# The recurrent solve in 64x64 blocks: one inverse per block pair instead of products on the right-hand sides

## What is computed

```python
def time_step(state, inp):            # state: 8 heads x 64 x 64
    rt, wt, ktt, vt, kht, at = inp
    sk = jnp.einsum('bhvk,bhk->bhv', state, kht)
    state = (state * wt[:, :, None, :]
             - sk[..., None] * (at * kht)[:, :, None, :]
             + vt[..., None] * ktt[:, :, None, :])
    return state, jnp.einsum('bhvk,bhk->bhv', state, rt)
...
_, y = lax.scan(time_step, state0, (tm(r), tm(w), tm(kt), tm(v), tm(kh), tm(a)))
```

## Time and profile before

| | us |
|---|---|
| median of 3 runs | 2790.49 (2789.77 to 2793.28) |
| the profiled execution, whole | 2793.99 |
| its span, first to last instruction | 2792.1 |
| TensorE busy in it | 2194.2 |
| VectorE busy | 660.1 |
| ScalarE busy | 368.9 |
| mean granted clock of TensorE | 0.894 |

### The profile page before, as it was taken

One profiled execution on the slowest core, in us unless ns is written; L12 is line 12 of the kernel. 1 busy time (PEld: TensorE's weight loads), 2 busy tenths in 40 slices (PEclk: granted clock), 3 DMA queues, 4 the chain that ended last, 5 costly groups with the idle time before them and its releaser, 6 DMA issues. The chain is left out here.

```text
span 2792.1 us, 31787 instructions
## 1 busy us (share of the span) xinstructions
PE 2194.2 (79%) x13296; PEld 1373.5 (49%) x13297; DVE 660.1 (24%) x1432; ACT 368.9 (13%) x743; POOL 59.4 (2%) x96
## 2 busy tenths in 40 slices
PE   7887769987769968899766666699688997666665
PEld 5563436653338647688422232286477884222222
DVE  4541114621111253453200000022532112000001
ACT  1510011510010031201100000000311011000000
POOL 0200000200000000000000000000000000000000
PEclk9999999999889989999888788899898998878887
DMA  9349997239993410286699999944100446999997
GB/s 389 121 186 428 428 428 322 91 138 429 428 428 153 165 60 1 99 334 246 275 428 428 429 428 428 427 181 155 56 1 1 157 154 286 427 428 428 429 428 314
DMA packets 55834, 779.42 MB, mean 279 GB/s; under 512 B 6840, under 2 KB 7096, under 8 KB 8120
## 3 DMA queue, kind: packets, MB, share of 16 engines
q1 hardware_dynamic: 55736, 778.02, 66.9%
HBM read 776.95 MB, written 1.05 MB: 279 GB/s over the span
## 5 line engine op out<-in xcount | busy, mean ns | idle before, releaser
L1747 PE MATMUL bank<-ring,arena 128*32 128x512 f32 x3136 | 498.3, 772 | 337.8 <-DMA ring<-in_w_exp 334.0
L1747 PEld LDWEIGHTS bank<-ring,arena 128*32 128x32 f32 x3136 | 101.6, 126 | 726.4 <-DMA ring<-in_w_exp 493.8
L1772 PE MATMUL bank<-ring,arena 128*32 128x512 f32 x1568 | 197.0, 641 | 70.1 <-DMA ring<-in_w_exp 47.3
L885 PE MATMUL bank<-xnT,ring 128*128 128x256 f32 x960 | 212.2, 384 | 9.5 <-ACT xnT L368 9.5
L1927 DVE TENSOR_TENSOR arena<-bank,arena 128x256 f32<-128x256 f32 (+1 forms) x33 | 18.3, 554 | 788.1 <-PE bank L1747 561.3
L885 PEld LDWEIGHTS bank<-xnT,ring 128*128 128x128 f32 x960 | 185.3, 193 | 36.9 <-issue 11.2
L1478 PE MATMUL bank<-xnT,ring 128*128 128x256 f32 x768 | 178.9, 387 | 10.3 <-PEq L1013 10.3
L1478 PEld LDWEIGHTS bank<-xnT,ring 128*128 128x128 f32 x768 | 149.5, 195 | 33.2 <-issue 11.9
L1717 PE MATMUL bank<-arena 128*128 128x256 f32 x592 | 145.8, 402 | 3.6 <-DVE arena L1938 3.6
L1717 PEld LDWEIGHTS bank<-arena 128*128 128x128 f32 x592 | 115.6, 201 | 63.1 <-issue 47.7
L1772 PEld LDWEIGHTS bank<-ring,arena 128*32 128x32 f32 x1568 | 50.6, 113 | 186.6 <-issue 96.2
(11 more groups left out here) (339 smaller groups left out, 2235.7 us busy)
## 6 DMA issues: line engine op xcount, KB each, us to landing
ring<-in_w_exp SPq DMA_DIRECT2D x288, 2048.0 KB, 25.7
arena<-in_w_ada SPq DMA_DIRECT2D x24, 2048.0 KB, 11.2
ring<-in_w_in SPq DMA_DIRECT2D x20, 2048.0 KB, 20.9
ring<-in_w_merge SPq DMA_DIRECT2D x18, 2048.0 KB, 8.2
ring<-in_w_o SPq DMA_DIRECT2D x8, 2048.0 KB, 11.6
ring<-in_w_conv SPq DMA_DIRECT2D x6, 2048.0 KB, 26.4
ring<-in_w_rest SPq DMA_DIRECT2D x2, 1696.0 KB, 26.1
small<-in_small SPq DMA_DIRECT2D x2, 1440.0 KB
```

The source lines that it names most:

```text
L885: last = nc.tensor.matmul(o[:, T * j:T * j + T], w[:, k, col:col + P], xnT[:, k, :], start=k == 0, stop=k == KT - 1)
L1747: last = nc.tensor.matmul(o[rows(e), :], Xw[:, k, rows(e)], ring[:, slot(n), at:at + MW], start=k == 0, stop=k == KT - 1)
L1772: last = nc.tensor.matmul(o[rows(e), :], hidT[:, j, rows(e)], ring[:, slot(n), at:at + MW], start=j == 0, stop=j == ft - 1)
```

## The change

The solve no longer goes by groups. A unit is now a head h and a half c of the token tile, that is 64 tokens (two chunks), and all matrices of a unit are 64x64 with 32x32 blocks on their diagonal. Half c lies on partitions 64c to 64c+63 for operands and for outputs. A step does all 16 units of a token tile, eight heads and two halves, and the two token tiles alternate.

The rounds no longer touch the right-hand sides. With G set to A - 1 (`less_unit`), a round r squares `low` and multiplies the transposed `low` with [power | G] side by side (`round_`, 64x128 in rounds 1 and 2), and VectorE copies the new power and adds the other half to G (`made`). After five rounds G is the negative inverse; `solved` applies it once, `finish` applies the queries' parts into one accumulation, and `turn_back` turns the finished tiles back with 16 transposes, whose results ScalarE copies to `y_rwkv` and VectorE adds to `qrT`. ScalarE also takes the values' products and half of the evacuations. `keys` and `values`, the products of `kdT`, lie between the rounds. Three masks and an unused table leave the constants and two masks and a unit of 64 columns come in; some operands now lie in `small`, behind and in what the stage before has used up. All other stages are as before.

TensorE, in the first solve before: the first group from its start to its second round.

```diff
-put("before", same & (p[:, None] < p[None, :]))
-put("upto", same & (p[:, None] <= p[None, :]))
-put("after", same & (p[:, None] > p[None, :]))
+at = (p % HD)[:, None]
+to = np.arange(HD)[None, :]
+same = at // CH == to // CH
+put("before_upto", np.concatenate([same & (at < to), same & (at <= to)], 1))
+put("past", same & (at > to))
+put("unit", at == to)
-put("start", np.tile((np.arange(T) % CH == 0)[None, :], (P, 1)))
...
-    masks = cst[:, CONST["before"][0]:CONST["upto"][1]]
-    groups = [(t, h) for t in range(TT) for h in (0, 4)]
...
-            for g, (t, h0) in enumerate(groups):
-                if g:
-                    pe.wait_ge(fin_taken, 2 * g)
-                    pe.wait_ge(pow_ready, 7 * g)
...
-                for r in range(5):
...
-                    if r < 4:
-                        b0 = 2 * (r % 2)
-                        for which in ((0, 1) if r < 3 else (1,)):
-                            for i in range(4):
-                                a, b = (top(i), low(i)) if which == 0 else (low(i), top(i))
-                                last = nc.tensor.matmul(bank[b0 + which][:, P * i:P * i + P], a, b, start=True, stop=True)
-                            last.then_inc(sq_done, 1)
-                    pe.wait_ge(x_ready, 6 * g + r + 1)
-                    for i in range(4):
...
-                        last = nc.tensor.matmul(o, top(i), X5[:, 4 * t + (h0 + i) // 2, :, i % 2, :], start=True, stop=True)
-                    last.then_inc(x_prod, 1)
...
+    b_pairs, k_pairs, b_masked, k_masked, unit_ready, low_made, top_made, low_ready, top_ready, g_ready = (
+        sem(f"sol_{n}") for n in ("bpairs", "kpairs", "bmasked", "kmasked", "unit", "lowmade", "topmade", "low", "top", "g"))
+    akv_made, akv_taken, x_made, x_act, x_dve, fin_made, fin_act, fin_dve, fin_turned = (
+        sem(f"sol_{n}") for n in ("akv", "akvtaken", "x", "xact", "xdve", "fin", "finact", "findve", "finturned"))
+    spare_at = SMALL2
+    def wide(x, n):
+        return x.rearrange("p (h s) -> p h s", h=n)
+    B1 = [ar(6144, HEADS, P), ar(16896, HEADS, P)]
+    K1 = [ar(13824, HEADS, P), wide(small[:, spare_at:spare_at + 1024], HEADS)]
+    low = [[ar(7168, HEADS, HD), ar(11776, HEADS, HD)], [wide(small[:, spare_at + 1024:spare_at + 1536], HEADS), ar(12288, HEADS, HD)]]
+    TG = [wide(small[:, 0:1024], HEADS), ar(8704, HEADS, P)]
+    fin = [small[:, 0:1024].rearrange("p (q d) -> p q d", q=4), ar(8704, 4, 2 * P)]
+    units = [(h, c) for h in range(HEADS) for c in range(2)]
+    def rows(c):
+        return slice(HD * c, HD * c + HD)
+    def part(h):
+        return slice(HD * (h % 2), HD * (h % 2) + HD)
+    def x_out(b, h, c):
+        at = 256 * (h // 2 % 2)
+        return bank[b + h // 4][rows(c), at:at + 256].rearrange("p (w i d) -> p w i d", w=2, i=2)[:, :, h % 2, :]
+            def tokens(t, c):
+                return slice(P * t + HD * c, P * t + HD * c + HD)
+            def pairs(t, x, banks):
+                for h, c in units:
+                    j = h // 2
+                    last = nc.tensor.matmul(bank[banks[h % 2]][rows(c), P * j:P * j + P], x[part(h), j, tokens(t, c)],
+                                            qrT[part(h), j, t, :, HD * c:HD * c + HD], start=True, stop=True)
+                return last
+            def lower(t):
+                for h, c in units:
+                    j = h // 2
+                    last = nc.tensor.matmul(bank[4 * t + 2 + h % 2][rows(c), HD * j:HD * j + HD], qrT[part(h), j, t, 0, HD * c:HD * c + HD],
+                                            bT[part(h), j, tokens(t, c)], start=True, stop=True)
+                return last
+            def round_(t, r):
+                top = B1[t] if r == 0 else TG[t]
+                lo = low[t][r % 2]
+                if r == 0:
+                    pe.wait_ge(b_masked, 4 * t + 4)
+                else:
+                    pe.wait_ge(low_ready, 2 * r - 1 + t)
+                    if r < 4:
+                        pe.wait_ge(top_ready, 2 * min(r, 3) - 1 + t)
+                if r < 4:
+                    for h, c in units:
+                        last = nc.tensor.matmul(bank[4 * t + 2][rows(c), HD * h:HD * h + HD], top[rows(c), h, 0:HD], lo[rows(c), h, :], start=True, stop=True)
+                    last.then_inc(low_made, 1)
+                if r == 1:
+                    pe.wait_ge(unit_ready, t + 1)
+                if r >= 2:
+                    pe.wait_ge(g_ready, 2 * (r - 2) + t + 1)
+                a, b = (0, HD) if r == 0 else (0, P) if r < 3 else (HD, P)
+                for h, c in units:
+                    at = P * (h % 4)
+                    last = nc.tensor.matmul(bank[4 * t + h // 4][rows(c), at + a:at + b], lo[rows(c), h, :], top[rows(c), h, a:b], start=True, stop=True)
+                last.then_inc(top_made, 1)
+            def keys(t):
+                if t == 0:
+                    pe.wait_ge(b_masked, 8)
+                else:
+                    pe.wait_ge(akv_taken, 1)
+                pairs(t, kdT, (3, 7)).then_inc(k_pairs, 1)
+            def values(t):
+                pe.wait_ge(k_masked, 2 * t + 2)
+                for h, c in units:
+                    last = nc.tensor.matmul(bank[4 * t + 3][rows(c), HD * h:HD * h + HD], K1[t][rows(c), h, 0:HD], Vtok[rows(c), t, HD * h:HD * h + HD],
+                last.then_inc(akv_made, 1)
+            def solved(t):
+                pe.wait_ge(g_ready, 7 + t)
+                pe.wait_ge(akv_taken, t + 1)
+                for h, c in units:
+                    last = nc.tensor.matmul(x_out(4 * t, h, c), TG[t][rows(c), h, HD:P], X5[rows(c), 4 * t + h // 2, :, h % 2, :], start=True, stop=True)
+                last.then_inc(x_made, 1)
+            def finish(t):
+                pe.wait_ge(x_act, t + 1)
+                pe.wait_ge(x_dve, t + 1)
+                pe.wait_ge(akv_taken, 2)
+                for h in range(HEADS):
+                    for c in range(2):
+                        nc.tensor.matmul(x_out(4 * t + 2, h, c), B1[t][rows(c), h, HD:P], X5[rows(c), 4 * t + h // 2, :, h % 2, :],
+                                         start=h % 4 == 0, stop=False, skip_group_check=True)
+                    for c in range(2):
+                        last = nc.tensor.matmul(x_out(4 * t + 2, h, c)[:, 1, :], K1[t][rows(c), h, HD:P], Vtok[rows(c), t, HD * h:HD * h + HD],
+                                                start=False, stop=True, skip_group_check=True)
+                last.then_inc(fin_made, 1)
+            def turn_back(t):
+                pe.wait_ge(fin_act, t + 1)
+                pe.wait_ge(fin_dve, t + 1)
+                for w in range(2):
+                    for j in range(MT):
+                        last = nc.tensor.transpose(bank[4 * t + w][:, P * j:P * j + P], fin[t][:, j, P * w:P * w + P], K("ident"))
+                last.then_inc(fin_turned, 1)
+            for t in range(TT):
+                pairs(t, bT, (4 * t, 4 * t + 1))
+                lower(t).then_inc(b_pairs, 1)
+            for r in range(5):
+                for t in range(TT):
+                    round_(t, r)
+                if r in (0, 2):
+                    keys(r // 2)
+                if r in (1, 3):
+                    values(r // 2)
+            for t in range(TT):
+                solved(t)
+            for t in range(TT):
+                finish(t)
+            for t in range(TT):
+                turn_back(t)
+            for r in range(4):
+                for t in range(TT):
+                    act.wait_ge(low_made, 2 * r + t + 1)
+                    nc.scalar.copy(low[t][(r + 1) % 2], wide(bank[4 * t + 2][:, :], HEADS)).then_inc(low_ready, 1)
+                if r in (1, 3):
+                    t = r // 2
+                    act.wait_ge(akv_made, t + 1)
+                    nc.scalar.copy(X[:, 4 * t:4 * t + 4, P:2 * P], wide(bank[4 * t + 3][:, :], 4)).then_inc(akv_taken, 1)
+            for t in range(TT):
+                act.wait_ge(x_made, t + 1)
+                nc.scalar.copy(X[:, 4 * t:4 * t + 2, :], wide(bank[4 * t][:, :], 2)).then_inc(x_act, 1)
+            for t in range(TT):
+                act.wait_ge(fin_made, t + 1)
+                nc.scalar.copy(fin[t][:, 0:2, :], wide(bank[4 * t + 2][:, :], 2)).then_inc(fin_act, 1)
+            for t in range(TT):
+                act.wait_ge(fin_turned, t + 1)
+                nc.scalar.copy(y_rwkv[:, :, P * t:P * t + P], wide(bank[4 * t + 1][:, :], MT))
+            def mask(dst, src, name, n, masked):
+                nc.vector.tensor_tensor(dst, wide(src, MT), K(name).unsqueeze(1).broadcast_to([P, MT, n]), ALU.mult).then_inc(masked, 1)
+            def masks_b(t):
+                dve.wait_ge(b_pairs, t + 1)
+                for p in range(2):
+                    mask(B1[t][:, p::2, :], bank[4 * t + p][:, :], "before_upto", P, b_masked)
+                for p in range(2):
+                    mask(low[t][0][:, p::2, :], bank[4 * t + 2 + p][:, 0:256], "past", HD, b_masked)
```

(53 more changed lines are left out.)

73 lines of the change are left out of this document (removed).

## The result

The changed kernel takes 2705.47 us (median of 4 runs, 2705.07 to 2706.16), beside 2791.89 us (2789.77 to 2796.45) for the kernel before: a ratio of 0.9689, 95% interval [0.9672, 0.9705]. The forecast was 2705 us with a range of 2687 to 2742. Two later groups of five runs on other occasions gave 0.9683 [0.9668, 0.9698] and 0.9681 [0.9668, 0.9694]. The profiled execution took 2705.52 us, its span is 2703.6.

What follows compares the result with a forecast made beforehand. TensorE bounds both recurrent solves; 39.1 + 0.8 + 1.9 + 1.7 + 0.5 = 44.0 us replaces 86.7 in each, saving 85.5, plus 0.3 for constants. From the 2790.49 median, minus 85.8: 2705 us, range 2687 to 2742.

Steps and rivals of the forecast that it cites:

- The bound: Both recurrent solves: TensorE busy 76 of 86.7 us each, no DMA; time saved there moves all that follows forward.
- The sum of a solve: New solve: 39.1 of TensorE work + 0.8 + 1.9 + 1.7 + 0.5 = 44.0 us against 86.7.
- 576 records of 64 columns on the diagonal: In each solve, 64x64 block products with both array halves at work: 31 ns a record, 17.9 us.
- 256 of 128 columns: In each solve, wider diagonal products priced from the old finish: 57 ns a record, 14.6 us.
- pairs and keys: In each solve, 128 records on all four array quarters at half the two-quarter price: 3.7 us.
- half a fall of the clock: In each solve, half of one fall of about 6.7 us beside the low start: 1.7 us charged.
- the low end of the range: No falls or supply cost, cheaper 128-column records, second layer's chain at full clock (5.6 us): 2691, with room 2687 us.
- The cost without the cover: In each solve, without the other token tile's cover, ten half rounds expose up to 1.5 us each, 15 us.
- A: Clock stays low for much of the new solve: whole solves at 1.2 GHz give 2776 us, half 2740; 14%.
- B: Solve's two halves can't write one bank at once: diagonal records cost double, +32.5 us a solve, 2770 us; 4%.
- C: Same halves of the diagonal block each other in the solve: 144 us a solve, 2905 us; 3%.
- D: Instruction supply in the solve: 8 or 9 packets at 1.79 us each, 14 us a solve, 2732 us; 5%.

## Why the prediction was right, and where it was off

**The bound.** That both solves were TensorE's and nothing behind them depended on their length held. DMA moves nothing to speak of in them, and at the same place as in rows 4 the first matmul of the merge of the kernel after waits again for the sequencer (5.32 us), not for weights. The saving moved everything forward.

**The sum of a solve.** Forecast 44.0 us, measured 40.9 and 40.8; the prediction's sign for a solve was 42 to 47 us, so both fell just below it. Term by term, with the measured prices of solve 1:
- 576 records of 64 columns on the diagonal, 31 ns forecast, 29 measured: 17.9 against 16.8 us;
- 256 of 128 columns, 57 forecast, 54.5 measured: 14.6 against 14.0. The nearest row, the finish, was the right one to lean on: 58 ns there;
- pairs and keys 3.7 against 3.9 (L1225's 32 records between 1059.19 and 1060.18, some 31 ns), lower products 1.0 against 1.2, with the wait of 0.3 in it: four quarters work at once;
- transposes and change of form 1.9 against 2.0;
- low clock at the start 1.9 against 1.95 (half of the 3.9 us up to 1054.4), the end 0.8 against 1.03.

That is 40.9. Two terms of the forecast have no counterpart: 1.7 us for half a fall of the clock and 0.5 us for instructions. The clock stood at the full level from 1054.4 to the end of the solve, and 8 packets of instructions came in time: there is no idle issue in it. These are the mis-sized terms, 2.2 of the 3.1 us.

**The clock.** The observation that the old solve falls behind a stretch with 1.75 us of work was read rightly, and the new one has no such stretch and no such fall. Charging half a fall all the same was caution. What the prediction left out is the chain. It let the chains only stay or get faster (it held 5.6 us of gain in the second open for the low end of the range); that the first could lose its full clock was not considered. This step was wrong: between the two profiled executions chain 1 took 6.7 us more and chain 2 0.7. Whether the change brought this about, or the full clock of chain 1 before was one draw, stays open: there is one trace of the kernel before, and the kernel with blocks only had falls in its solves and in both chains. The gain of 6.3 us by which the solves beat their forecast is nearly the same size as these 7.5 us; that the median fell so close to 2705 is in part luck: two misses that nearly cancel.

**The other stages.** The start, the stage between the first head norm and the second solve, and the end hold the same work; they gave -4.2 us in sum. The middle took 866.8 us before and 864.0 with blocks only, and with the whole change 858.5, 858.4 and 861.3 in three traces of the same kernel. In all twelve traces with the changed solve, the experiments' included, it took 858.4 to 862.1 us. That is 2 to 8 us less than in the two traces with the old one. Part of it stands at the very start of the stage: the first matmul of the merge starts 11.2 us behind that of the head norm before (rows 4 and 10) and 9.85 now; the head norm's first row took 3.60 us then, at the lower clock, and takes 1.96 now, at the full one. The cause of the rest stays open.

**The waits and the hiding work.** VectorE was forecast at 22.6 us and has 21.8, ScalarE 9.3 and 9.4; TensorE's waits on VectorE, forecast at 0.9 us hidden, are up to 0.3 us. The cost without the cover was put at up to 15 us a solve, the experiment gave 9.8. So the part of the schedule in the gain was rightly seen and overrated by a third.

**The rivals.** A (low clock through the solve) is out: 0.95 and 0.96. B (the halves can't write one bank at once) is out at 29 ns, where it would be about 60. The Trainium skill, TensorEngine Tiling (Array Packing), Restrictions and Gotchas, has the rule that different row tiles cannot access the same PSUM bank simultaneously; in this kernel the two halves write different partitions of one bank, record by record, at 29 ns each, so the measurement decides against applying it here. C (the products of one half block each other) needed 72 ns a record; even the order made to bring it about came to some 46 (29 x 1.58). D (instruction supply) has nothing in the solve.

## What to carry to other kernels

A block-diagonal product at full array width pays for its zeros: two 64x64 blocks, issued in turn, took 58 ns for both where the 128x128 record took 110. But take the order into account at once: the blocks in the rounds alone brought 12 of 46 us, and with runs on one half of the array 16 us of the gain are lost again, without the alternation of the token tiles 10 (these figures overlap and don't add up). Look also at small products that use another part of the array than their neighbour: those with the values took 0.18 us a record and gave 8 us of the gain (that the change of part was the cause is not shown). And put the clock of the stages around into the range of a forecast: the same chain took 19.5 us in one trace and 23.9 to 27.0 in the others, with or without a fall.

## What the hardware showed that was not expected

In runs of one half of the array the cost was 1.58 times that of the alternating order, not 2, and records of two products appear interleaved at the seam (rows of the experiment with runs of one half). The trace of the changed kernel has such a place too, from 1071.62, where records of the keys' product (L1225) start between the last ones of a round's (L1256).

The clock's falls depend on something that the traces read here don't show. TensorE at the full level ahead of the first solve bought 0.3 us in it (40.5 against 40.8), since the lower level came back 1.0 us into it; two executions of one chain with the same program, records and nearly the same idle time ran at 20.7 and at 26.1 us.
